# Hybrid attention and mixture-of-experts layer: queries without rotation projected straight to features

## The reference

```python
cq_n = rms_norm(cq, q_norm_g)                                  # (tokens, 256)
q = (cq_n @ w_uq).reshape(B, Tp, DSA_HEADS, QK_NOPE_DIM + QK_ROPE_DIM)   # 8 heads x (64 + 32)
q_nope, q_rope = q[..., :QK_NOPE_DIM], rope(q[..., QK_NOPE_DIM:], pos)
q_idx = rope_partial((cq_n @ w_qidx).reshape(B, Tp, IDX_HEADS, IDX_HEAD_DIM), pos, IDX_ROPE_DIM)   # 4 x 64
```

## Time and profile before

| | before |
|---|---|
| median of 3 runs | 1147.63 us (1146.41 to 1148.13) |
| profiled execution | 1146.74 us, span 1144.9 us |
| PE busy | 1095.6 us, 96% |
| DVE busy | 335.2 us, 29% |
| ACT busy | 214.6 us, 19% |
| POOL busy | 14.6 us, 1% |
| moved by DMA | 433.60 MB, mean 379 GB/s |

### The profile page before, as it was taken

How to read it: one execution, slowest core, us unless ns; L and a number is a source line. 1 busy time by engine, 2 the same in 40 slices (tenths; PEclk the granted TensorE clock), 3 DMA queues, 4 the chain that set the end, 5 groups by cost and what they waited for, 6 DMA issues and landing times. The chain is left out here.

```text
span 1144.9 us, 13669 instructions
## 1 busy us (share of the span) xinstructions
PE 1095.6 (96%) x5458; PEld 519.8 (45%) x5458; DVE 335.2 (29%) x827; ACT 214.6 (19%) x391; POOL 14.6 (1%) x29
## 2 busy tenths in 40 slices
PE   8999999999999999898989898989999999999997
PEld 7868888454343434343434343434343434343433
DVE  2285552132313222222222213131322231322223
ACT  3438880131101110111111101010111100111012
POOL 3010000000000000000000000000000000000000
PEclk9999999999999999999999999999999989999999
DMA  9914229879999999999999999999999999999996
GB/s 309 289 37 147 96 89 378 344 302 432 430 430 434 429 435 428 434 433 429 436 427 435 428 434 434 428 436 427 435 426 422 428 433 429 433 430 427 426 419 249
DMA packets 39858, 433.60 MB, mean 379 GB/s; under 512 B 3144, under 2 KB 19938, under 8 KB 24340
## 3 DMA queue, kind: packets, MB, share of 16 engines
q1 hardware_dynamic: 38464, 430.11, 89.8%
q0 software_dynamic: 960, 2.30, 0.6%
q10 hardware_dynamic: 404, 0.79, 0.2%
HBM read 432.13 MB, written 1.05 MB: 378 GB/s over the span
## 5 line engine op out<-in xcount | busy, mean ns | idle before, releaser
L1954 PE MATMUL psum<-arena 128*64 128x512 f32 x880 | 199.9, 608 | 7.9 <-DMA arena<-in_w_gate_up 7.9
L1954 PE MATMUL psum<-ring,arena 128*64 128x512 f32 x824 | 186.0, 604 | 6.9 <-DMA ring<-in_w_gate_up 6.9
L1328 DVE TENSOR_TENSOR arena<-psum,biasT 128x512 f32<-128x512 f32 x64 | 44.2, 691 | 297.0 <-PE psum L1896 292.6
L1971 PE MATMUL psum<-ring,arena 128*64 128x512 f32 x544 | 121.4, 596 | 9.7 <-DMA ring<-in_w_down 9.5
L1954 PEld LDWEIGHTS psum<-arena 128*64 128x64 f32 x880 | 62.0, 139 | 137.9 <-issue 123.4
L961 DVE TENSOR_TENSOR arena<-psum,vT 128x512 f32<-128x512 f32 (+2 forms) x43 | 28.5, 668 | 327.8 <-PE psum L1823 320.7
L1971 PE MATMUL psum<-arena 128*64 128x512 f32 x480 | 106.5, 595 | 10.6 <-DMA arena<-in_w_down 10.6
L1954 PEld LDWEIGHTS psum<-ring,arena 128*64 128x64 f32 x824 | 57.3, 138 | 126.5 <-issue 114.0
L872 ACT ACTIVATE arena<-psum 128x1024 f32<-128x1024 f32 x32 | 32.7, 1023 | 325.1 <-PE psum L1927 219.4
L1352 DVE TENSOR_TENSOR h<-h,psum 128x1024 f32<-128x1024 f32 x62 | 72.9, 1217 | 15.0 <-PE psum L1996 12.9
L1971 PEld LDWEIGHTS psum<-ring,arena 128*64 128x64 f32 x544 | 40.8, 137 | 79.8 <-issue 74.1
(11 more groups left out here) (256 smaller groups left out, 838.8 us busy)
## 6 DMA issues: line engine op xcount, KB each, us to landing
arena<-in_w_gate_up SPq DMA_DIRECT2D x28, 4096.0 KB, 28.5
ring<-in_w_gate_up SPq DMA_DIRECT2D x25, 4096.0 KB, 28.8
ring<-in_w_down SPq DMA_DIRECT2D x14, 4096.0 KB, 27.8
arena<-in_w_down SPq DMA_DIRECT2D x13, 4096.0 KB, 29.8
ring<-in_w_gate_up SPq DMA_DIRECT2D x9, 2048.0 KB, 26.5
ring<-in_w_in SPq DMA_DIRECT2D x14, 1024.0 KB, 12.9
arena<-in_w_gate_up SPq DMA_DIRECT2D x6, 2048.0 KB, 24.5
arena<-in_w_gate_up SPq DMA_DIRECT2D x8, 1024.0 KB, 30.0
```

Of the source, the lines that this page charges most:

```text
L1328: return v.tensor_tensor(dst.rearrange("p (m j) -> p m j", m=8), src, bias[:, m:m + 8, cols(e, 1)].broadcast_to([P, 8, CAP]), ALU.add)
L1954: ins = mm(bank[home + n][h * CAP:(h + 1) * CAP, :], xg[:, c, e * CAP:(e + 1) * CAP], part, start=c == 0, stop=c == CH - 1)
L1971: ins = mm(bank[home][n * CAP:(n + 1) * CAP, :], rows[:, c * CAP:(c + 1) * CAP], w[:, n * 512:(n + 1) * 512], start=first, stop=last)
```

## The change

The unrotated 64 columns of each head are no longer projected by token and transposed. They are projected with the weights as the stationary operand, so that the result comes by feature: for each pair of heads a bank holds one head in partitions 0 to 63 and the other in 64 to 127, over 256 tokens, and ACT copies both into `qcat` with `two_heads_out`. By token remain the 8 x 32 rotated columns and the 256 index columns, together 512 for each tile, in one bank each. The rotated columns are transposed four heads at a time (two transposes for each tile), and ACT copies them in four pieces of 32 rows for each tile. DVE rotates the same data, now packed. The number of jobs is the same: 4 + 4 before, 6 + 2 after, with those between moved two places.

```diff
-    jobs += [("q", t, n) for t in range(2) for n in range(2)]
+    jobs += [("qr", t) for t in range(2)]
+    jobs += [("qn", k) for k in range(4)]
...
-    jobs += [("qT", t, n) for t in range(2) for n in range(2)]
+    jobs += [("rT", t) for t in range(2)]
...
+        wuq = wq[:, :, 0:HEADS * QK].rearrange("p c (h n) -> p c h n", n=QK)
...
+        qrope = qcat.rearrange("p (b q k) -> p q b k", b=2, q=4)
...
             for t in range(2):
-                for n in range(2):
-                    copy_out(("q", t, n), qtok[:, t, n * 512:(n + 1) * 512], job_bank(("q", t, n))[:])
+                copy_out(("qr", t), qtok[:, t, 0:512], job_bank(("qr", t))[:])
+            for k in range(4):
+                two_heads_out(("qn", k), qcat, k, SEQ)
...
             for t in range(2):
-                for n in range(2):
-                    copy_out(("qT", t, n), qcat[0:QK, 4 * n:4 * n + 4, t * P:(t + 1) * P],
-                             job_bank(("qT", t, n))[0:QK, :].rearrange("p (h k) -> p h k", h=4))
+                wait_filled(sc, ("rT", t))
+                for m in range(4):
+                    ins = sc.activation(qrope[NOPE:QK, m, :, t * P:(t + 1) * P],
+                                        job_bank(("rT", t))[m * ROPE:(m + 1) * ROPE, 0:2 * P]
+                                        .rearrange("p (b k) -> p b k", b=2), ACT.Copy)
+                empty_end(ins, ("rT", t))
...
             for t in range(2):
-                for n in range(2):
-                    wait_emptied(dve, ("q", t, n))
-                for n, (o, heads, per, off) in enumerate(((768, IH, ID, 0), (0, HEADS, QK, NOPE))):
+                wait_emptied(dve, ("qr", t))
+                for n, (o, heads, per, off) in enumerate(((HEADS * ROPE, IH, ID, 0), (0, HEADS, ROPE, 0))):
...
             for t in range(2):
-                for n in range(2):
-                    name = ("q", t, n)
-                    fill_begin(pe, name)
-                    for c in range(2):
-                        ins = mm(job_bank(name)[:], cqT[:, c, t * P:(t + 1) * P],
-                                 wq[:, c, n * 512:(n + 1) * 512], start=c == 0, stop=c == 1)
-                    fill_end(ins, name)
+                name = ("qr", t)
+                fill_begin(pe, name)
+                for c in range(2):
+                    mm(job_bank(name)[:, 0:256].rearrange("p (h n) -> p h n", h=HEADS), cqT[:, c, t * P:(t + 1) * P],
+                       wuq[:, c, :, NOPE:QK], start=c == 0, stop=False)
+                    ins = mm(job_bank(name)[:, 256:512], cqT[:, c, t * P:(t + 1) * P], wq[:, c, HEADS * QK:1024],
+                             start=False, stop=c == 1)
+                fill_end(ins, name)
+            for k in range(4):
+                name = ("qn", k)
+                fill_begin(pe, name)
+                for c in range(2):
+                    for u in range(2):
+                        ins = mm(job_bank(name)[u * NOPE:(u + 1) * NOPE, 0:SEQ], wuq[:, c, 2 * k + u, 0:NOPE],
+                                 cqT[:, c, :], start=c == 0, stop=c == 1)
+                fill_end(ins, name)
...
             for t in range(2):
-                for n in range(2):
-                    name = ("qT", t, n)
-                    fill_begin(pe, name)
-                    for h in range(4):
-                        ins = tr(job_bank(name)[0:QK, h * P:(h + 1) * P],
-                                 qtok[:, t, (4 * n + h) * QK:(4 * n + h + 1) * QK], ident)
-                    fill_end(ins, name)
+                name = ("rT", t)
+                fill_begin(pe, name)
+                if t == 0:
+                    pe.wait_ge(s_qr, 4)
+                for b in range(2):
+                    ins = tr(job_bank(name)[:, b * P:(b + 1) * P], qtok[:, t, b * P:(b + 1) * P], ident)
+                fill_end(ins, name)
...
                     if h == 0:
-                        for n in range(2):
-                            wait_emptied(pe, ("qT", t, n))
+                        wait_emptied(pe, ("rT", t))
+                        for k in range(4):
+                            wait_emptied(pe, ("qn", k))
```

More of the change, by code:

```diff
@@ L1616, in index_queries @@
                     ins = tr(job_bank(name)[:, k * P:(k + 1) * P],
-                             qtok[:, t, 768 + 2 * k * ID:768 + 2 * (k + 1) * ID], ident)
+                             qtok[:, t, HEADS * ROPE + 2 * k * ID:HEADS * ROPE + 2 * (k + 1) * ID], ident)
                 fill_end(ins, name)
```

## The result

| | before | changed |
|---|---|---|
| median of 22 runs | 1147.11 us | 1149.2 us |
| lowest and highest | 1145.78 to 1149.73 | 1147.4 to 1150.82 |
| profiled execution, span | 1146.74, 1144.9 | 1149.12, 1147.3 |

The ratio is 1.0016, 95% interval 1.0010 to 1.0022: 1.8 us slower (1.1 to 2.5), which is inside the range and about halfway between the forecast of +1.0 and rival B's +2.7; the 2.3 us that I had set as the limit of what can be told lies inside the interval.

What follows compares the result with a forecast made beforehand. PE was taken to set the start of a fixed-length expert-weight stream. Values 0.45 us later and ACT copies +1.17 us outweighed -1.34 us of transposes on PE: +1.00 us on 1147.63, so 1148.6 us, range 1146.2 to 1150.6.

Steps and rivals of the forecast that it cites:

- rival B: PE's wait at the first transposed probabilities lets its granted clock fall: +2.7 us, 1150.3 us; chance 0.12.
- What bounds the kernel: PE, busy from 90 to 241 us, sets the start of a fixed-length expert-weight stream; early delays pass one for one.
- The projections: Query projections on PE: 6.97 us removed, 7.01 us added, plus 0.15 us for changes between full and half width.
- Rival C: Half-width matmuls don't run side by side, or pieces of 32 read at half rate: +4.5 or +2.7 us; chance 0.05.
- The copies behind them: ACT's copies after the projections: index-query copy 0.30 us later, so values begin 0.45 us later, width change included.
- The copies of the transposes: On ACT, eight 32 x 256 copies (3.12 us) replace four of 96 x 512 (1.95 us): +1.17 us.
- the strips: ACT's token-strip copies, quarter after quarter of one bank without overlap; taken as the model, 0.39 us per new copy.
- the sum: First exponential at 93.99 instead of 92.37 us, PE's first transposed probabilities at 95.22 instead of 94.22: +1.00 us.
- The wait: PE, there at 93.33 us, waits 1.9 us for ACT at the first transposed probabilities, eating the transposes' gain.
- Rival A: PE is the bound all through and the fewer transposes count: -0.9 us, 1146.7 us; chance 0.08.
- Rival D: Some later wait takes up the lag, so it never reaches the end: 0, 1147.6 us; chance 0.10.
- The level: The whole kernel's forecast time of 1148.6 us, counted from a median of 1147.63 us.

Runs made afterwards that it cites:

- e3_act3: The kernel before with three more ACT copies of 32 x 256 behind the last query copy, into columns nothing reads; ratio to before 1.0008 (0.9999 to 1.0018).
- e1_pad: The changed kernel with 12 transposes of no use behind its four, in a bank nothing reads; median 1148.01 us, ratio to before 1.0010 (1.0002 to 1.0019).
- e9_more: The changed kernel with two more ACT copies of 32 x 256 behind the last of the eight; ratio to before 1.0021 (1.0011 to 1.0031).

## Why the prediction was right, and where it was short

- **What bounds the kernel.** Right. Every kernel's loss or gain at the first expert weights was there again, within 0.03 us, at the start of the steady stream, but for e3_act3, whose clock fell in between. From there to the end of the span the profiled executions took 903.8 to 904.7 us (before 903.8), so that part is as long as it is only to within 0.9 us; what sets this difference isn't shown.
- **The projections.** Forecast 7.16 us (7.01 and 0.15 for the width); 64.87 - 57.62 = 7.25. The full-width ones took 61.27 - 57.62 = 3.65 instead of 3.50, so reading pieces of 32 costs next to nothing, and the half-width ones 64.87 - 61.27 = 3.60 instead of 3.51, so two of them do run side by side. Rival C falls.
- **The copies behind them.** Forecast values 0.45 us later; 10.88 against 10.37 us from the first projection: 0.51. Two misses nearly cancel in it: the projections are 7.25 - 6.97 = 0.28 of it (forecast 0.15), and what is left for the copies is 0.23 (forecast 0.30).
- **The copies of the transposes.** Forecast 3.12 us; 89.98 - 86.87 = 3.11. The choice to go by the strips and the two-head copies, which don't overlap, was the one that carried the sum. By the overlap of the Trainium skill (ScalarE: Activation LUTs, What ACT_TABLE_LOAD costs) an estimate is 2.45 us; the trace, with 3.11, doesn't agree for copies that change partitions. The prediction's remark that by such an overlap the stall would nearly vanish doesn't follow from its own rows: PE at 94.22 + 0.15 - 1.34 = 93.03 would still have waited 1.2 us for data at 94.25. Only the total of about 0 does.
- **The wait.** Forecast 1.9 us and probabilities +1.00 us; 1.75 and +1.13, the same to 0.01 us in all four executions. e1_pad and e3_act3 show it from both sides: PE's work there is free, ACT's is not. Rival A falls. With the clock up, the loss at the first expert weights is 1.21 us (forecast 1.00). Rival D falls too.
- **The level.** The forecast of 1148.6 us stands on a median of three runs, which lay 0.5 us above that of all 22. On 1147.11 the same +1.00 gives 1148.1, so that the stated time comes as near to 1149.2 as it does is in part luck.
- **What was short.** Without a fall of the clock the loss was 1.21 us at the first expert weights, not 1.00. With one it was 2.90, near rival B's +2.7. I set the fall as an alternative to the forecast, at 0.12. It is an event that strikes some executions of one and the same kernel, one of four profiled, and costs 1.69 us (forecast 1.7). That the wait brings it isn't shown. For it: between 90 and 110 us the clock fell in two of the five executions with a wait of 1.74 us or more (the second is e9_more) and in none of the seven with 0.43 us or less. Against it: so few executions can fall out like that by chance, and in e3_act3 it fell behind waits of 0.22 us and less. The medians' +1.8 us (1.1 to 2.5) lies between the two values, 1.2 and 2.9, and its interval reaches down to the first, so the timed runs don't show that falls are part of it. How often the clock fell in them isn't shown either, since they have no profile by stage: 6 of the 22 took less than 1148 us, as the three executions without a fall did, but the kernel before scatters over 4 us as well.

## What to carry to other kernels

Before work is taken from an engine that looks fully busy, look at how long ago its next datum was ready: here 0.7 us, so at most that much could be gained, and a few more instructions on the other engine turned the gain into a loss. When a wide copy is cut into narrow ones from different partitions, count each at its full duration. Where an engine off the path has a gap, look also at which job could move so that the gap becomes long enough: the kernel with the same eight copies on VectorE reached the first expert weights 0.84 us later before the projections were moved than after, and moving them gave only 0.14 us of this where just four copies were on VectorE.

## What the runs showed of the hardware

- A PE wait of 1.75 us in the midst of dense matmuls was followed by half the clock (1.2 GHz) for some 3.4 us in one execution of a program, and waits of 1.74 us at the same place by no fall in three others. In the kernel before the shortest idle time looked at that had a fall behind it was 2.3 us; in e3_act3 a fall came behind waits of 0.16 and 0.22 us. What brings a fall stays open.
- Eight ACT copies of 32 x 256, each from another quarter of the partitions, took 3.11 us, 0.39 each, their full duration (0.38 to 0.39), where full-height copies of 272 columns start 0.32 apart.
- A VectorE copy of 32 x 256 from PSUM takes 0.44 us (eight in 3.48 us), more than the 0.39 us of ACT's, which I had not expected.
